# FFN block pairs of a two-block transformer kernel: seven half-width products in place of eight for the last eight pairs of eleven

## Chip, cores and metric

One core of one Trainium2 chip. The metric is the device time of one launch in microseconds, the median over runs. A TensorE clock has two levels here, 1.2 and 2.4 GHz; the profile gives the granted share of the upper.

## What is computed

The reference runs 512 tokens of width 1024 in float32 through two transformer blocks: a hybrid mixer, cross attention and an FFN, then an FFN, a recurrent mixer, cross attention and an FFN again. Three stages have the form that the change touches:

```python
def rms_norm(x, g):
    y = x * lax.rsqrt(jnp.mean(x * x, axis=-1, keepdims=True) + EPS)
    return y * g
def swiglu(h, w_gate, w_up, w_down):        # w_gate, w_up: 1024 x 2816, w_down: 2816 x 1024
    return (silu(h @ w_gate) * (h @ w_up)) @ w_down
# fa: x = x + swiglu(rms_norm(x)); fb, fc: x = x + 0.5 * swiglu(rms_norm(x))
```

## The kernel before

Everything is kept transposed: a tile has 128 features on the partitions and the 512 tokens along the row. Float32 accuracy comes from splitting each operand into a high part in a rounded format (`whi`, `xh`, `hh`) and the rest (`wlo`, `xl`, `hl`); each product is three matmuls, high x high, high x low and low x high, all issued at line 1170 and summed in one PSUM bank.

The weights pass in slots of 256 rows by 512 columns through four buffers each of `raw`, `whi` and `wlo`. `load` (line 2917) fetches a slot on SP's queue, `w_hi` on ScalarE rounds it (line 1541 is the helper that records it), `w_lo` on VectorE subtracts (helper line 2030). Python code writes one order list, `ORDER`, from which each engine's program is made; `gemm` (line 405) runs over the slots of one weight group and its four output tiles, `point` and `soon` (lines 367 and 363) place the work of the other engines between the matmul groups, and `Counts` turns each event into a semaphore value. PSUM has eight banks: `main` (0 to 3) for the large products and `side` (4 to 7) for the rest.

An FFN stage (`ffn`, line 935) has eleven block pairs. Pair i takes 256 gate and 256 up columns: four slots, four output tiles, 2 x 3 matmuls of 512 columns in each. `ffn_gate` on VectorE (line 2500) multiplies the gate sum by `R`, the norm factor of each token; ScalarE (line 1884) takes the Silu; GpSimd (line 2842, helper 2764) multiplies by `R` once more for the up half; `ffn_up` on VectorE (line 2508) multiplies by the up sum; ScalarE (line 1889) and `h_lo` (line 2515) split the hidden tile. Two products of 22 deep tiles, `d0` and `d1`, bring it back to width 1024; `residual` adds them to `xT`. The gain is folded into `xh` and `xl`, and `R` of a stage comes from squares, a sum on GpSimd and two small TensorE products (line 1265) in its first pair. In fb the residual stream itself is normalised as well, by `x_scaled` (line 2521).

The printed code below also shows the memory projections' weight groups (`mkv1`, `mkv2`), whose tokens are 256 and whose matmuls therefore have 256 columns.

## Time and profile before

| what | us |
|---|---|
| timed runs | 2422.54, 2423.30, 2423.92 (median 2423.3) |
| profiled execution, span from first to last instruction | 2420.5 |
| mean granted TensorE clock | 0.998 |
| busy: TensorE, VectorE, ScalarE, GpSimd | 2397.5, 1263.9, 1002.5, 331.9 |
| the three FFN stages in the chain | 362.3, 353.2, 347.1 |
| DMA traffic | 251.65 MB, mean 104 GB/s |

The profiled execution is a fourth one; of it the profile gives the span, and no time around the span is listed. In the views, PE is TensorE's matmuls and PEld its weight loads (they overlap matmuls), DVE is VectorE, ACT ScalarE, POOL GpSimd, SPq SyncE's DMA queue. A matmul's printed duration reaches into the next one; its cost is the distance between starts. "idle before" is the engine's idle time ahead of a group and what ended it.

### The profile page before, as it was taken

How to read it: one execution, taken by the hardware profiler on the slowest of the kernel's cores; microseconds unless marked ns; L12 is line 12 of the kernel's file. 1: busy time of each engine (PE TensorE's matmuls, PEld its weight loads, DVE VectorE, ACT ScalarE, POOL GpSimd, SP SyncE). 2: the span in 40 equal slices, each digit the busy share in tenths (PEclk: the TensorE clock that was granted, in tenths of full speed). 3: DMA queues.
4: the chain of work that ended last, by engine and by line, in shares of the span. 5: the costliest groups of instructions: out<-in, count | busy, mean ns of one | idle time of the engine just before them, and what ended most of it. 6: DMA issues, size and time to landing. Idle time of an engine off the chain costs nothing.

```text
span 2420.5 us, 30412 instructions
## 1 busy us (share of the span) xinstructions
PE 2397.5 (99%) x12064; PEld 1956.4 (81%) x12064; DVE 1263.9 (52%) x1907; ACT 1002.5 (41%) x1634; POOL 331.9 (14%) x258
## 2 busy tenths in 40 slices
PE   8999999999999999999999999999999999999998
PEld 7777778777898888888888888888887888888887
DVE  5688746468765455443333544333678555333422
ACT  7766654234563344333223433222644454323321
POOL 0000000555100100111102111101032201101100
PEclk9999999999999999999999999999999999999999
DMA  6221235323665232332323332332322232333231
GB/s 203 71 70 51 86 99 183 113 68 108 200 210 209 96 105 70 105 95 88 96 97 101 99 97 90 96 100 88 111 63 63 87 113 74 101 96 105 97 100 56
DMA packets 172638, 251.65 MB, mean 104 GB/s; under 512 B 11472, under 2 KB 90576, under 8 KB 172496
## 3 DMA queue, kind: packets, MB, share of 16 engines
q1 hardware_dynamic: 171344, 248.13, 32.5%
q8 instruction: 95, 1.56, 0.3%
q10 hardware_dynamic: 1152, 1.57, 0.2%
q14 instruction: 47, 0.39, 0.1%
HBM read 231.83 MB, written 16.78 MB: 103 GB/s over the span
## 4 chain that ended last, share of the span: by engine, by line
PE 96%; DVE 2%; ACT 1%; issue 0%; POOL 0%; DMA 0%; DVEq 0%; SPq 0%; POOLq 0%
PE bank L1170 94%; PE bank L1299 1%; DVE wlo L2030 0%; PE bank L1322 0%; DVE T L2038 0%; PE bank L1447 0%; PE bank L1423 0%; DVE macc L2030 0%; PE bank L1265 0%; DMA raw<-in_w_in 0%; DVE xg L2034 0%; ACT whi L1541 0%; DVE ml L2038 0%; DVE bank L2336 0%; DVE W L2030 0%
## 5 line engine op out<-in xcount | busy, mean ns | idle before, releaser
L1170 PE MATMUL bank<-xh,whi 128*128 128x512 f32 x1784 | 710.1, 398 | 8.0 <-DVE wlo L2030 8.0
L1170 PE MATMUL bank<-xh,wlo 128*128 128x512 f32 x1784 | 696.6, 390 | 0.0
L1170 PE MATMUL bank<-xl,whi 128*128 128x512 f32 x1784 | 695.9, 390 | 0.0
L2030 DVE TENSOR_TENSOR wlo<-raw,whi 128x1024 fp32r<-128x1024 f32 (+2 forms) x406 | 500.2, 1234 | 337.2 <-ACT whi L1541 337.0
L1541 ACT ACTIVATE whi<-raw 128x1024 fp32r<-128x1024 f32 (+2 forms) x406 | 419.2, 1038 | 513.7 <-PE bank L1170 507.2
L1170 PEld LDWEIGHTS bank<-xh,whi 128*128 128x128 f32 x1784 | 335.7, 188 | 94.7 <-issue 20.2
L1170 PEld LDWEIGHTS bank<-xh,wlo 128*128 128x128 f32 x1784 | 335.4, 188 | 71.1
L1170 PEld LDWEIGHTS bank<-xl,whi 128*128 128x128 f32 x1784 | 336.0, 188 | 65.4
L2030 DVE TENSOR_TENSOR T<-bank,R 128x512 f32<-128x512 f32 x86 | 59.0, 687 | 344.3 <-PE bank L1170 344.3
L1170 PE MATMUL bank<-hh,whi 128*128 128x512 f32 (+1 forms) x536 | 206.9, 386 | 0.0
L1170 PE MATMUL bank<-hl,whi 128*128 128x512 f32 (+1 forms) x536 | 206.8, 386 | 0.0
L1170 PE MATMUL bank<-hh,wlo 128*128 128x512 f32 (+1 forms) x536 | 206.8, 386 | 0.0
L2764 POOL TENSOR_TENSOR T<-T,R 128x512 f32<-128x512 f32 x66 | 94.0, 1424 | 618.6 <-ACT T L1887 618.6
L1887 ACT ACTIVATE T<-T 128x512 f32<-128x512 f32 x66 | 41.7, 632 | 235.0 <-DVE T L2030 235.0
L1170 PEld LDWEIGHTS bank<-hh,whi 128*128 128x128 f32 x536 | 100.7, 188 | 20.5
L1170 PEld LDWEIGHTS bank<-hh,wlo 128*128 128x128 f32 x536 | 100.7, 188 | 20.4
L1170 PEld LDWEIGHTS bank<-hl,whi 128*128 128x128 f32 x536 | 100.7, 188 | 20.0
L2764 POOL TENSOR_TENSOR acc<-acc,T 128x512 f32<-128x512 f32 (+1 forms) x43 | 62.9, 1462 | 227.0 <-ACT T L1595 170.9
L1170 PE MATMUL bank<-whi,xh 128*128 128x512 f32 (+1 forms) x192 | 90.2, 470 | 0.0
L2764 POOL TENSOR_TENSOR xw<-xg,sm 128x512 f32<-128x512 f32 x24 | 28.6, 1201 | 446.1 <-DVE T L2030 421.0
L2785 POOL COPY acc<-T 128x512 f32<-128x512 f32 x8 | 5.5, 692 | 553.1 <-ACT T L1595 553.1
L1784 ACT ACTIVATE E<-bank,sm 128x128 f32<-128x128 f32 x128 | 40.0, 365 | 95.0 <-DVE bank L2336 72.4
(356 smaller groups left out, 3494.9 us busy)
## 6 DMA issues: line engine op xcount, KB each, us to landing
raw<-in_w_in SPq DMA_DIRECT2D x92, 512.0 KB, 3.6
raw<-in_w_ffn_in SPq DMA_DIRECT2D x88, 256.0 KB, 3.2
raw<-in_ffn_gate SPq DMA_DIRECT2D x88, 256.0 KB, 2.8
raw<-in_ffn_up SPq DMA_DIRECT2D x88, 256.0 KB, 3.1
raw<-in_ffn_down SPq DMA_DIRECT2D x44, 512.0 KB, 3.6
raw<-in_w_ffn_out SPq DMA_DIRECT2D x22, 512.0 KB, 3.6
raw<-in_w_xattn_kv SPq DMA_DIRECT2D x16, 512.0 KB, 4.4
raw<-in_w_kv_mem SPq DMA_DIRECT2D x16, 512.0 KB, 4.9
```

What stands on the lines that cost most here:

```text
L1170: return e.matmul(out, l, r, start=start, stop=stop, skip_group_check=skip)
L1299: ins = e.transpose(b[:, chunk(r)], p[:, r, chunk(j)], ident)
L1541: return e.activation(out, in_, ACT.Copy)
L1784: ins = e.activation(E[n % 3][:, c, :], b[:, chunk(j)], ACT.Exp, bias=nac[:, c, 32 + n:33 + n])
L1887: e.activation(t[:], t[:], ACT.Silu).then_inc(*up("ffn_silu", ("ffn silu", tag, j)))
L2030: return e.tensor_tensor(out, a, b, op)
L2764: return e.tensor_tensor(out, a, b, op)
L2785: e.tensor_copy(sums[:, 0:width], t[:, 0:width]).then_inc(*up("sum_pool", ("sum", tag, k), ("tmp", "free", n)))
```

## The change

The first three pairs of each stage (`PLAIN`) stay as they are. For the other eight, weights (1024 x 512 for gate and up together) are cut in two by output columns (128 and 128 of each tile pair) and in two by depth (even and odd tiles of 128), tokens in two halves of 256. The eight quarter products are then had from seven, with sums of weight quarters and of token quarters as operands and the products summed in PSUM in a shared order.

- Weights: a quarter (`quarter`, 1 MB, gate and up, one depth parity) is loaded by two DMAs (`load_quarter`). VectorE forms four combinations a pair (`w_sum`), ScalarE and VectorE split seven operands of 1024 elements a partition (`s_hi`, `s_lo`).
- Tokens: `operands` builds, during the three plain pairs, seven token operands of 256 columns in high and low form for each of four depth pairs (`x_gain`, `x_norm`, `x_sum`, `op_hi`, `op_lo`). They hold gain and `R`, so nothing is multiplied by `R` afterwards, and GpSimd has no part in these pairs.
- Products: `product` runs 2 x 4 x 3 matmuls of 256 columns. The order (`product_order`) weaves a pair's last three among the next pair's first four. Product 1 is copied from bank a to bank b (`seed_b`), so that two sums go on from it; a second copy (`seed_f`) follows product 7; products 5 and 6 are kept in SBUF (`keep`) and added later (`c22`, `c12`). Pairs alternate between the `main` and `side` banks and between two rings of four temporary tiles.
- Silu and multiplication go by quarters of 256 tokens (`s_silu`, `s_mul`) into `hid`. The split of all 22 hidden tiles (`split_h`) moves from the pairs to the end of the products and into `d0`; `x_scaled` moves into `d0`.
- The GpSimd DMA scratch is 1 KB, so all tiles start lower in SBUF. `hh`, `hl`, `quarter`, `shi`, `slo` and `xop` share space with `xh`, `xl`, `raw`, `whi` and `wlo`, which adds waits at the start and end of the products.

```diff
-        hh = [at_kb(118 + 2 * j, [P, S], F32R, name="hh") for j in range(22)]
-        hl = [at_kb(162 + 2 * j, [P, S], F32R, name="hl") for j in range(22)]
+        HH = [218, 96, 98, 100, 102] + [162 + 2 * j for j in range(17)]
+        hid = [at_kb(118 + 2 * j, [P, S], name="hid") for j in range(22)]
+        hl = [at_kb(118 + 2 * j, [P, S], F32R, name="hl") for j in range(22)]
+        hh = [at_kb(kb, [P, S], F32R, name="hh") for kb in HH]
+        quarter = [at_kb(kb, [P, 2, 4, 256], name="quarter") for kb in (0, 8, 72, 80)]
+        wsum = [at_kb(kb, [P, 2, 4, P], name="wsum") for kb in (88, 92)]
+        shi = [at_kb(16 + 4 * i, [P, 2, 4, P], F32R, name="shi") for i in range(NH)]
+        slo = [at_kb(32 + 4 * i, [P, 2, 4, P], F32R, name="slo") for i in range(NH)]
+        xop = [at_kb(162 + 14 * i, [P, 14, 256], name="xop") for i in range(4)]
+        xopr = [at_kb(162 + 14 * i, [P, 14, 256], F32R, name="xopr") for i in range(4)]
 
...
+        def product_order():
+            order = [(PLAIN, p) for p in (1, 5, 6, 2)]
+            for i in range(PLAIN + 1, 11):
+                order += [(i - 1, 7), (i, 1), (i - 1, 4), (i, 5)]
+                order += [(i - 1, 3), (i, 6), (i, 2)]
+            return order + [(10, 7), (10, 3), (10, 4)]
+        PRODUCTS = product_order()
+        PLACE = {x: n for n, x in enumerate(PRODUCTS)}
+        COMBINED = {5: 0, 6: 1}
...
+        def seven_finished(tag, i, p):
+            if p == 1:
+                step("seed_b", tag, i)
+            elif p in (5, 6):
+                step("keep", tag, i, p)
+            elif p == 2:
+                step("s_silu", tag, i, 11)
+                soon(0, "s_mul", tag, i, 11)
+            elif p == 7:
+                step("seed_f", tag, i)
+                step("c22", tag, i)
+                soon(0, "s_silu", tag, i, 22)
+                soon(1, "s_mul", tag, i, 22)
+            elif p == 4:
+                step("s_silu", tag, i, 21)
+                soon(0, "s_mul", tag, i, 21)
+            elif p == 3:
+                step("c12", tag, i)
+                soon(0, "s_silu", tag, i, 12)
+                soon(1, "s_mul", tag, i, 12)
+        def prepare_sum(tag, n):
+            if n < len(PRODUCTS) and PRODUCTS[n][1] in (5, 6, 7):
+                step("w_sum", tag, *PRODUCTS[n])
+        def prepare_last(tag, n):
+            if n < len(PRODUCTS) and PRODUCTS[n][1] == 3:
+                step("w_sum", tag, *PRODUCTS[n])
+        def prepare_hi(tag, n):
+            if n < len(PRODUCTS):
+                step("s_hi", tag, n)
+                soon(0, "s_lo", tag, n)
...
+        def split_h(tag, j):
+            step("h_hi", tag, j)
+            soon(0, "h_lo", tag, j)
+        def begin_seven(tag):
+            def hook(n):
+                if n == 4:
+                    for i in range(PLAIN, 11):
+                        for e in range(2):
+                            step("quarter", tag, i, e)
+                if n in (11, 13, 15):
+                    prepare_hi(tag, (n - 11) // 2)
+                if n in (12, 14):
+                    prepare_sum(tag, n // 2 - 5)
+            return hook
+        def seven(tag):
+            first = SEVEN[tag] + len(PRODUCTS)
+            ready[0] = loaded[0] = first
+            upto[0] = min([x for x in SEVEN.values() if x > first] + [NS])
+            for n, (i, p) in enumerate(PRODUCTS):
+                ring = seven_ring(i)[0]
+                if p == 1:
+                    for b, letter in enumerate("aebf"):
+                        ring.new(letter, tag, i, among=(b,))
+                    for b, what in enumerate(("even", "odd", "c22", "u2")):
+                        (tmp2 if i % 2 else tmp).new(what, tag, i, among=(b,))
+                step("product", tag, n)
+                pay()
+                owed.append(lambda i=i, p=p: seven_finished(tag, i, p))
+                point()
+                prepare_sum(tag, n + 4)
+                prepare_last(tag, n + 6)
+                prepare_hi(tag, n + 3)
+                if (i, p) == (8, 5):
+                    split_h(tag, 0)
+                if n >= PLACE[9, 3] + 3:
+                    split_h(tag, n - PLACE[9, 3] - 2)
+                if n + 3 >= len(PRODUCTS):
+                    split_to(first + n + 4 - len(PRODUCTS))
+            step("mark", f"{tag}d")
...
+            drain(built[0])
+            seven(tag)
+            for x, j in enumerate(range(4, 22)):
+                soon(max(0, 2 * x - 2), split_h, tag, j)
+            if tag == "fb":
+                for k in range(8):
+                    soon(4 + 4 * k, "x_scaled", k)
...
+            def product(tag, n):
+                i, p = PRODUCTS[n]
+                c = SEVEN[tag] + n
+                h, l = shi[c % NH], slo[c % NH]
+                letter = {1: "a", 2: "a", 5: "e", 3: "e", 6: "b", 7: "b", 4: "f"}[p]
+                hi, lo = {1: (11, 4), 2: (12, 5), 3: (13, 6), 4: (10, 3), 5: (7, 0), 6: (9, 2), 7: (8, 1)}[p]
+                u, b = seven_bank(letter, tag, i)
+                w.wait_ge(*at("w lo", c))
+                if p in (1, 5):
+                    ring, name = seven_ring(i)
+                    w.wait_ge(*free(ring, name, u))
+                elif p in (2, 6):
+                    w.wait_ge(*at("seed b", tag, i))
+                elif p == 7:
+                    w.wait_ge(*at("kept", tag, i, 6))
+                elif p == 4:
+                    w.wait_ge(*at("seed f", tag, i))
+                else:
+                    w.wait_ge(*at("kept", tag, i, 5))
+                for gu in range(2):
+                    out = b[:, 256 * gu:256 * gu + 256]
+                    for k in range(4):
+                        w.wait_ge(*at("op lo", tag, k, 0 if hi > 10 else 1))
+                        a, d = h[:, gu, k, :], l[:, gu, k, :]
+                        t, tl = xopr[k][:, hi, :], xopr[k][:, lo, :]
+                        mm(out, a, t, p in (1, 5) and gu == 0 and k == 0, False, skip=True)
+                        mm(out, a, tl, False, False, skip=True)
+                        ins = mm(out, d, t, False, k == 3, skip=True)
+                ins.then_inc(*up("gemm", ("product", tag, i, p), ("w used", c)))
...
+            def op_hi(tag, kp, part):
+                t, tr = xop[kp], xopr[kp]
+                if part == 0:
+                    w.wait_ge(*at("x norm", tag, kp))
+                    ins = copy(tr[:, 11:14, :], t[:, 8:11, :])
+                else:
+                    w.wait_ge(*at("x sum", tag, kp))
+                    w.wait_ge(*at("op lo", tag, kp, 0))
+                    ins = copy(tr[:, 7:11, :], t[:, 0:4, :])
+                ins.then_inc(*up("x_hi", ("op hi", tag, kp, part)))
+            def s_hi(tag, n):
+                i, p = PRODUCTS[n]
+                c = SEVEN[tag] + n
+                if p in (1, 2, 4):
+                    w.wait_ge(*at("quarter", tag, i, 0 if p == 1 else 1))
+                else:
+                    w.wait_ge(*at("w sum", tag, i, p))
+                w.wait_ge(*at("w used", c - NH))
+                copy(eight(shi[c % NH][:]), part_of(tag, i, p)).then_inc(*up("w_hi", ("w hi", c)))
+            def seed_b(tag, i):
+                ring, name = seven_ring(i)
+                u, b = seven_bank("b", tag, i)
+                w.wait_ge(*free(ring, name, u))
+                w.wait_ge(*at("product", tag, i, 1))
+                copy(b[:], seven_bank("a", tag, i)[1][:]).then_inc(*up("x_exp", ("seed b", tag, i)))
+            def keep(tag, i, p):
+                name, n, t = seven_tile("c22" if p == 5 else "u2", tag, i)
+                w.wait_ge(*free(tmp2 if i % 2 else tmp, name, n))
+                w.wait_ge(*at("product", tag, i, p))
+                copy(t[:], seven_bank("e" if p == 5 else "b", tag, i)[1][:]).then_inc(*up("x_exp", ("kept", tag, i, p)))
+            def seed_f(tag, i):
+                ring, name = seven_ring(i)
+                u, f = seven_bank("f", tag, i)
+                w.wait_ge(*free(ring, name, u))
+                w.wait_ge(*at("product", tag, i, 7))
+                copy(f[:], seven_bank("b", tag, i)[1][:]).then_inc(*up("x_exp", ("seed f", tag, i)))
...
+            def x_norm(tag, kp):
+                t = xop[kp]
+                w.wait_ge(*at("R", "fb2" if tag == "fb" else tag))
+                w.wait_ge(*at("x gain", tag, kp))
+                r0, r1 = (R[:, o:o + 256].unsqueeze(1).to_broadcast([P, 2, 256]) for o in (0, 256))
+                tt(t[:, 8:10, :], t[:, 8:10, :], r0, ALU.mult)
+                tt(t[:, 7:11:3, :], t[:, 7:11:3, :], r1, ALU.mult).then_inc(*up("x_lo", ("x norm", tag, kp)))
+            def x_sum(tag, kp):
+                t = xop[kp]
+                w.wait_ge(*at("x norm", tag, kp))
+                tt(t[:, 0:2, :], t[:, 7:8, :].to_broadcast([P, 2, 256]), t[:, 8:11:2, :], ALU.subtract).then_inc(
+                    *up("x_lo", ("x first", tag, kp)))
+                w.wait_ge(*at("x first", tag, kp))
+                tt(t[:, 2, :], t[:, 10, :], t[:, 0, :], ALU.subtract).then_inc(*up("x_lo", ("x second", tag, kp)))
+                w.wait_ge(*at("x second", tag, kp))
+                tt(t[:, 3, :], t[:, 9, :], t[:, 2, :], ALU.subtract).then_inc(*up("x_lo", ("x sum", tag, kp)))
...
+            def w_sum(tag, i, p):
+                out = part_of(tag, i, p)
+                w.wait_ge(*at("quarter", tag, i, 0))
+                w.wait_ge(*at("quarter", tag, i, 1))
+                if p in COMBINED:
+                    if i == PLAIN:
+                        w.wait_ge(*at("w used", G[f"{tag}{PLAIN - 1}"]["ids"][1]))
+                    else:
+                        w.wait_ge(*at("w hi", slot_of(tag, i - 1, p)))
+                        w.wait_ge(*at("w lo", slot_of(tag, i - 1, p)))
+                        w.wait_ge(*at("w sum", tag, i - 1, 6 if p == 5 else 3))
+                if p == 5:
+                    ins = tt(out, part_of(tag, i, 7), part_of(tag, i, 4), ALU.add)
+                elif p == 6:
+                    w.wait_ge(*at("w sum", tag, i, 5))
+                    ins = tt(out, part_of(tag, i, 5), part_of(tag, i, 1), ALU.subtract)
+                elif p == 7:
+                    w.wait_ge(*at("w sum", tag, i, 5))
+                    ins = tt(out, out, part_of(tag, i, 1), ALU.subtract)
+                else:
+                    there = slot_of(tag, i, 5 if i == 10 else 2)
+                    w.wait_ge(*at("w hi", there))
+                    w.wait_ge(*at("w lo", there))
+                    w.wait_ge(*at("w sum", tag, i, 6))
+                    ins = tt(out, part_of(tag, i, 2), part_of(tag, i, 6), ALU.subtract)
+                ins.then_inc(*up("w_lo", ("w sum", tag, i, p)))
+            def s_lo(tag, n):
+                i, p = PRODUCTS[n]
+                c = SEVEN[tag] + n
+                w.wait_ge(*at("w hi", c))
+                tt(eight(slo[c % NH][:]), part_of(tag, i, p), eight(shi[c % NH][:]).bitcast(F32), ALU.subtract).then_inc(
+                    *up("w_lo", ("w lo", c)))
+            def c22(tag, i):
+                t = seven_tile("c22", tag, i)[2]
+                u, b = seven_bank("b", tag, i)
+                w.wait_ge(*at("kept", tag, i, 5))
+                w.wait_ge(*at("seed f", tag, i))
+                tt(t[:], b[:], t[:], ALU.add).then_inc(*up("ffn_in", ("c22", tag, i), (seven_ring(i)[1], "free", u)))
+            def c12(tag, i):
+                t = seven_tile("u2", tag, i)[2]
+                u, x = seven_bank("e", tag, i)
+                w.wait_ge(*at("kept", tag, i, 6))
+                w.wait_ge(*at("product", tag, i, 3))
+                tt(t[:], x[:], t[:], ALU.add).then_inc(*up("ffn_in", ("c12", tag, i), (seven_ring(i)[1], "free", u)))
...
+            def load_quarter(tag, i, e_):
+                r = quarter_of(i, e_)
+                ids = G[f"{tag}{PLAIN - 1}"]["ids"]
+                before = [(j, x) for j in range(PLAIN, 11) for x in range(2) if (j, x) < (i, e_) and quarter_of(j, x) == r]
+                if before:
+                    for event in quarter_done(tag, *before[-1]):
+                        w.wait_ge(*event)
+                elif r > 1:
+                    w.wait_ge(*at("w used", ids[2 * r - 3]))
+                else:
+                    for c in ids:
+                        if c % NR // 2 == r:
+                            w.wait_ge(*at("w hi", c))
+                            w.wait_ge(*at("w lo", c))
+                for gu, (src, c0) in enumerate(SOURCE[tag]):
+                    e.dma_start(quarter[r][:, gu, :, :], src[:, c0 + 256 * i:c0 + 256 * i + 256].rearrange(
+                        "(k e p) n -> p k e n", e=2, p=P)[:, :, e_, :]).then_inc(
+                        *up(f"mx{r}", *([("quarter", tag, i, e_)] if gu else [])))
 
...
```

## Rows read from the trace of the kernel before

**Rows 1.** The page: span, busy time of each engine, granted clock by slice, chain

```profile
span 2420.5 us, 30412 instructions
PE 2397.5 (99%) x12064; PEld 1956.4 (81%) x12064; DVE 1263.9 (52%) x1907; ACT 1002.5 (41%) x1634; POOL 331.9 (14%) x258
...
PEclk9999999999999999999999999999999999999999
...
PE 96%; DVE 2%; ACT 1%; issue 0%; POOL 0%; DMA 0%; DVEq 0%; SPq 0%; POOLq 0%
```

**Rows 2.** The chain in order of time (start us, us, what), the FFN stages

```profile
985.50 362.28 PE bank L1170 x1606
...
1354.13 353.23 PE bank L1170 x1562
...
2064.01 347.12 PE bank L1170 x1560
```

**Rows 3.** Timeline of TensorE in an FFN block (start us, us, engine, line, operation)

```profile
1000.11 0.39 PE L1170 MATMUL bank<-xh,wlo 128*128 128x512 f32 x1
...
1002.83 0.39 PE L1170 MATMUL bank<-xh,wlo 128*128 128x512 f32 x1
```

**Rows 4.** Timeline of TensorE in the memory projections, 256 columns

```profile
625.33 0.28 PE L1170 MATMUL bank<-ml,whi 128*128 128x256 f32 x1
...
627.97 0.28 PE L1170 MATMUL bank<-mh,wlo 128*128 128x256 f32 x1
```

**Rows 5.** Timeline of TensorE's weight loads beside rows 4

```profile
625.33 0.19 PEld L1170 LDWEIGHTS bank<-mh,wlo 128*128 128x128 f32 x1
625.45 0.19 PEld L1170 LDWEIGHTS bank<-mh,whi 128*128 128x128 f32 x1
```

**Rows 6.** Timeline of VectorE at the end of an FFN block

```profile
1017.12 1.22 DVE L2030 TENSOR_TENSOR wlo<-raw,whi 128x1024 fp32r<-128x1024 f32 x1
1018.25 0.68 DVE L2030 TENSOR_TENSOR hl<-T,hh 128x512 fp32r<-128x512 f32 x1
1018.86 1.22 DVE L2030 TENSOR_TENSOR wlo<-raw,whi 128x1024 fp32r<-128x1024 f32 x1
```

**Rows 7.** Groups of VectorE by form (busy us, mean ns, idle before)

```profile
L2030 DVE TENSOR_TENSOR wlo<-raw,whi 128x1024 fp32r<-128x1024 f32 x394 | 493.2, 1254 | 331.2 <-ACT whi L1541 331.0
L2030 DVE TENSOR_TENSOR T<-bank,R 128x512 f32<-128x512 f32 x86 | 59.0, 687 | 344.3 <-PE bank L1170 344.3
L2038 DVE SCALAR_TENSOR_TENSOR xl<-xT,vec,xh 128x512 fp32r<-128x512 f32 x48 | 52.7, 1106 | 4.9 <-ACT xh L1542 4.9
L2336 DVE COPY_PREDICATED bank<-cst,bank 128x256 f32<-128x256 int32 x64 | 26.8, 420 | 1.7 <-PE bank L1170 1.6
```

**Rows 8.** Groups of ScalarE by form

```profile
L1541 ACT ACTIVATE whi<-raw 128x1024 fp32r<-128x1024 f32 x394 | 412.7, 1053 | 510.4 <-PE bank L1170 505.3 <-DMA raw<-in_w_branch_ssd 4.7
L1541 ACT ACTIVATE hh<-T 128x512 fp32r<-128x512 f32 x66 | 41.6, 630 | 24.5 <-DVE T L2030 24.5
L1541 ACT ACTIVATE pt<-bank 128x512 f32<-128x512 f32 x40 | 23.3, 585 | 17.2 <-PE bank L1299 17.1
L1541 ACT ACTIVATE q<-bank 128x256 f32<-128x256 f32 x16 | 6.0, 378 | 19.8 <-PE bank L1170 19.8
```

**Rows 9.** Groups of GpSimd by form

```profile
L2764 POOL TENSOR_TENSOR T<-T,R 128x512 f32<-128x512 f32 x66 | 94.0, 1424 | 618.6 <-ACT T L1887 618.6
```

**Rows 10.** Busy time by stretch: us, PE, PEld, DVE, ACT, POOL, clock, DMA share, GB/s

```profile
979.30:1348.20 368.90, 368.90 (x1641) 305.83 (x1641) 140.41 (x160) 112.79 (x141) 53.26 (x36) 1.00 0.31 97
640.00:660.00 20.00, 20.00 (x128) 16.77 (x128) 15.74 (x29) 15.15 (x34) 0.40 (x1) 1.00 0.83 265
```

**Rows 11.** DMA issues of the page (count, KB each, us to landing)

```profile
raw<-in_w_ffn_in SPq DMA_DIRECT2D x88, 256.0 KB, 3.2
...
raw<-in_ffn_down SPq DMA_DIRECT2D x44, 512.0 KB, 3.6
```

**Rows 12.** The chain in order of time, memory projections beside the scan

```profile
618.50 60.38 PE bank L1170 x498
```

More of the change, by code:

```diff
@@ L13 @@
 S = 512
-BASE = 17408
+SCRATCH = 1024
+BASE = SCRATCH + 1024
 EPS = 1e-6
@@ L213, in build @@
         tmp = Ring([at_kb(104 + i * 2, [P, S], name="T") for i in range(4)])
+        tmp2 = Ring([at_kb(96 + i * 2, [P, S], name="T2") for i in range(4)])
         zb = Ring([at_kb(kb, [P, S], name="zb") for kb in (154, 156)])
@@ L369, in point @@
             delayed[:] = [[d[0] - 1, d[1]] for d in delayed if d[0]]
-            for d in sorted(due, key=lambda d: d[1][0] != "w_lo"):
+            for d in sorted(due, key=lambda d: d[1][0] not in ("w_lo", "s_lo")):
                 if callable(d[1][0]):
@@ L935, in ffn, with build @@
         def ffn(tag, out):
+            built = []
+            def build():
+                built.append(start(operands(tag), 3))
             if tag == "fb":
@@ L950, in scale @@
                             step("spread", "fb")
-                            for k in range(8):
-                                soon(1 + 2 * k, "x_scaled", k)
                         soon(3, scale)
@@ L956, in ffn, with ahead @@
             else:
-                later(1, norm(tag))
+                def ahead():
+                    norm(tag)()
+                    soon(5, build)
+                later(1, ahead)
             step("mark", f"{tag}")
-            for i in range(11):
+            for i in range(PLAIN):
                 def evict(m, i=i):
@@ L1887, in ffn_gate, with h_hi @@
                 e.activation(t[:], t[:], ACT.Silu).then_inc(*up("ffn_silu", ("ffn silu", tag, j)))
-            def ffn_up(tag, j):
-                n, t = tmp("gate", tag, j)
+            def h_hi(tag, j):
+                w.wait_ge(*at("h done", tag, j))
+                if 0 < j < 5:
+                    for q in (11, 22, 21, 12):
+                        w.wait_ge(*at("s mul", tag, 9, q))
+                elif j > 4:
+                    w.wait_ge(*at("product", tag, 10, 3))
+                copy(hh[j][:], hid[j][:]).then_inc(*up("h_hi", ("h hi", tag, j)))
@@ L2013, in scalar @@
                     "mv_out": mv_out, "kv_split": kv_split, "xq_out": xq_out, "x_scores": x_scores, "x_turn": x_turn, "x_pv": x_pv, "ffn_gate": ffn_gate,
-                    "ffn_up": ffn_up, "bounds": bounds, "f_sig": f_sig, "f_log": f_log, "h_silu": h_silu,
+                    "h_hi": h_hi, "x_gain": x_gain, "op_hi": op_hi, "s_hi": s_hi, "seed_b": seed_b, "keep": keep, "seed_f": seed_f,
+                    "s_silu": s_silu, "bounds": bounds, "f_sig": f_sig, "f_log": f_log, "h_silu": h_silu,
                     "i_out": i_out, "u_first": u_first, "b_split": b_split, "level": level, "ends": ends, "ke_turn": ke_turn,
@@ L2747, in vector @@
                     "ffn_gate": ffn_gate, "ffn_up": ffn_up, "h_lo": h_lo, "x_scaled": x_scaled, "residual": residual,
+                    "x_norm": x_norm, "x_sum": x_sum, "op_lo": op_lo, "w_sum": w_sum, "s_lo": s_lo, "c22": c22, "c12": c12, "s_mul": s_mul,
                     "bounds": bounds, "f_out": f_out, "f_gate": f_gate, "f_log": f_log, "h_out": h_out,
```

169 lines of the change are left out of this document (141 added, 28 removed).

## The prediction

> **What bounds the kernel now.** I read the page first. TensorE is busy for 99% of a span of 2420.5 us, its granted clock stands in the top tenth in all forty slices, and 96% of the chain that ended last is TensorE's own [rows 1]. The chain in order of time then shows the three feed-forward (FFN) stages, fa, fb and fc, as unbroken runs of TensorE work: 362.3, 353.2 and 347.1 us, with nothing but norm matmuls between them [rows 2]. So in these stages only TensorE's own work counts, and whatever takes from it is gained one for one until another engine makes it wait.
>
> What one matmul costs must be read from starts, since the page's means (some 390 ns) overlap. In an FFN block a matmul of 512 columns starts every 2.72/12 = 0.2267 us [rows 3]. Where the moving operand has 256 columns, in the memory projections, one starts every 2.64/22 = 0.120 us [rows 4], and each has its own weight load, started at the same distance [rows 5]. A half-width matmul thus costs 53% of a full one, not 50%: 106.7 ns for 256 columns at the granted full level of 2.4 GHz and 13.3 ns beside it; 213.3 and 13.3 for 512.
>
> **TensorE's part.** A block pair (256 gate and 256 up columns, 1024 deep, 512 tokens) is now 4 weight slots x 4 output tiles x 2 x 3 = 96 matmuls of 512 columns, 96 x 0.2267 = 21.76 us. In the new form it is 7 products x 2 (gate, up) x 4 deep tiles x 3 = 168 matmuls of 256 columns, 168 x 0.120 = 20.16 us. That is 7/8 of the columns (6144 fewer, 2.56 us) with 72 more of the fixed 13.3 ns (0.96 us): 1.60 us less. Eight pairs in each of three stages: 24 x 1.60 = 38.4 us.
>
> The Trainium skill's page "TensorE: Matmul & The Clock Gate", section "Back-to-back issue gap", gives N/2.4 + 2.5 ns a matmul, so 215.8 and 109.2 ns; by it, as an estimate, a pair would gain 2.37 us and all of them 57 us. The rows have 226.7 and 120.0, and the measurement decides.
>
> **What must keep pace.** Each product waits for a high and low half of its own weight combination (`s_hi` on ScalarE, `s_lo` on VectorE), and four of seven for a combination that VectorE first adds up (`w_sum`).
> - VectorE, per pair: four `w_lo` of 1024 elements, two `ffn_gate` and two `ffn_up` go, two `h_lo` move to the down product; seven `s_lo`, four `w_sum` (all 1024 elements), `c22` and `c12` (512) and four `s_mul` (256) come. From start to start a 1024-element operation takes 1.13 us and a 512-element one 0.61 [rows 6]; 256 elements I put at 0.34 (0.61 less the 0.27 us between the 687 and 420 ns forms [rows 7]). 11 x 1.13 + 2 x 0.61 + 4 x 0.34 = 15.0 us of 20.16, 74%. Taken with the full mean durations, 11 x 1.254 + 2 x 0.69 + 4 x 0.42 = 16.9 us, 84%. The sums read 128-column pieces, which no row shows; I take the plain price.
> - ScalarE, per pair: seven `s_hi`, four copies of 512 (`seed_b` and `seed_f` from bank to bank, `keep` twice out of PSUM) and four Silu of 256 come, four `w_hi`, two Silu of 512 and two `h_hi` go or move. 7 x 1.053 + 4 x 0.585 + 4 x 0.378 = 11.2 us, 56% [rows 8]. No row has ScalarE writing PSUM. Bounds: the 585 ns of reading PSUM, and twice it; I take 0.6 us, as writing PSUM costs VectorE nothing unusual, 420 ns for 256 elements [rows 7].
> - GpSimd loses two multiplications by R a pair (1424 ns each), and with them the hop VectorE, ScalarE, GpSimd, VectorE at each eviction. It is off TensorE's path, so it gives nothing [rows 9].
> - Loads: the bytes are the same, 2 MB a pair, in 1 KB pieces as before; the FFN stage draws 97 GB/s with the DMA engines 31% busy, while another stretch of this kernel draws 265 [rows 10].
>
> **Do the waits bite?** I followed the order list by products of 2.88 us. `s_lo` of product n+2 stands in VectorE's queue behind only what product n-1's end releases, so it has nearly two products to run; the dearest such turn holds `c22` (0.6 us, and up to 0.9 us until `seed_f` has landed), one `s_lo` and one `w_sum`, 3.8 us, and the next two are short (1.5 and 2.6). A seed or a kept copy always has one whole product between what it reads and who needs it (6, then 2, then 7; 7, then 1, then 4): 2.88 us against about 1 us, even 1.5 with the dear copy. A quarter of weights (1 MB, two DMAs on SP's queue) comes free about 8.5 products into a pair's life and the sum that reads its successor comes at 12: 3.5 products or 10 us. SP's sixteen quarters a stage stand in one queue, each waiting in turn. A 256 KB piece lands in 3.2 us and one of 512 KB in 3.6 [rows 11]; two of these, even one after the other, are 7.2 us. If the quarter were late, `w_sum` would block VectorE and the `s_lo` behind it, with two more products before TensorE feels it. Steady state: no stall, 0 us.
>
> **Edges, three times each.** Token operands: four groups of scaling, sums and splits, 3840 elements on VectorE and 2816 on ScalarE each, so about 4 x 4.3 = 17 and 4 x 2.9 = 12 us, spread over the three plain blocks (65 us), where VectorE is busy 38% and ScalarE 31% of the time [rows 10]: hidden. At their price uncovered this would be 17 us a stage. Entry: the second pair's last quarter can only load once the last plain block has left `xl` and `xh`, and its first sum comes 3 products (8.6 us) on against at most 7.2: hidden by 1.4 us. Exit: the first down slot's `w_lo` runs in the last product behind `c12`: 0.2 + 0.6 + 1.13 us against 2.88, thin. The 18 remaining splits of hidden tiles (0.63 us on ScalarE, 0.61 on VectorE [rows 6, 8]) come about ten matmul groups ahead of use within 60 us of the first down product; the move of `x_scaled` there adds 8 x 0.8 us to VectorE and is hidden the same way. I take 0.6 us an edge pair, about 2 us in all; bounds 0 and 10.
>
> Sum against the profiled span: 2420.5 - 38.4 + 2 = 2384.1 us. The median of the runs, 2423.3, lies 2.8 us above that span, so 2386.9; I say 2387. Less than 0.2%, about 5 us, can't be told from no change here.
>
> **Rivals.**
> 1. The hand-overs bite. What would do it is a copy into PSUM while TensorE writes a neighbouring bank, or a VectorE queue that runs behind. The trace of before has no such copy and no such chain. At 0.2 to 1.3 us a pair the gain shrinks by 5 to 31 us: 2392 to 2418, middle 2400. A 0.1 us hole a product would already be 17 us. Chance 0.17.
> 2. VectorE becomes the bound and the kernel is slower. The place is the eleven 1024-element operations a pair. With the waits in the queue (about 2 us of `seed_f` and Silu landings) and 2.6 us of short ones, a pair exceeds the old 21.76 us when each costs over (21.76 - 4.6)/11 = 1.56 us. The mean today is 1.254 at longest [rows 7] and only `xl`'s operations of 512 elements show such slowness beside GpSimd work (1106 ns mean where 512 elements usually take 690). At 1.8 us a pair takes 24.4 us: + 2.6 x 24 = 63, so 2486. For it speaks the unseen strided read; against it that GpSimd falls silent in just these blocks. Chance 0.06.
> 3. Weight loads show. The load counts 188 to 192 ns in the trace [rows 5] and there are 168 where 96 were; if they ran one behind another a pair would take 31.6 us and the kernel 2423.3 + 24 x 9.8 = 2659 us. Against it: rows 5 have loads starting each 0.12 us, and 498 matmuls in 60.4 us (0.121 each) ran unbroken in the chain [rows 12], so neither loads nor instruction supply fail at that rate. Chance 0.02. The Trainium skill's page "TensorE: Matmul & The Clock Gate", section "Measured speedup vs the span model", says a load overlaps a matmul in flight only where the row group differs; by it this rival would hold. The trace disagrees: in rows 4 and 5 loads on all 128 rows start together with matmuls.
> 4. The change doesn't do what it says in time: the half-width gain is eaten to within 5 us of nothing (1.4 to 1.8 us of stall a pair, or an entry and exit stall of 10 to 13 us a stage). Chance 0.04.
>
> The forecast itself, 2383 to 2391, has 0.71.
>
> **Numbers.** Faster: forecast and rival 1, 0.88. Same 0.04, slower 0.08 (rivals 2, 3). The range runs from 2382 (edges free, pitch 0.1195 as the shortest 256-column stretches allow, 2 us) to 2402, which takes in the forecast and the better half of rival 1, and leaves out some 0.18.
>
> **What would show it.** Right: 4032 matmuls of 256 columns with `xop` as moving operand, 0.120 us apart; VectorE 70 to 85% busy in those stretches, ScalarE 50 to 60%; the chain still one run of TensorE per stage, some 12.8 us shorter each; pair to pair 20.2 us. Rival 1: idle of TensorE before `xop` matmuls released by ScalarE's `bank<-bank` copies. Rival 2: the same released by `slo`, with VectorE above 95%. Wrong altogether: a matmul pitch off 0.120, a granted clock below full, or `quarter` loads at the head of the waits.

## The result and the profile after

The changed kernel takes 2385.36 us (median, 2385.11 to 2385.97), the kernel before 2422.92 in the same comparison: ratio 0.9846, 95% interval 0.9832 to 0.9860. The forecast was 2387 in a range of 2382 to 2402. The profiled execution took 2385.45 us in all, 1.85 us more than its span.

The page after, for [rows 1]:

```profile
span 2383.6 us, 34351 instructions
PE 2359.7 (99%) x13792; PEld 2007.5 (84%) x13792; DVE 1525.4 (64%) x2207; ACT 1167.8 (49%) x1910; POOL 266.8 (11%) x210
...
PEclk9999999999999999999999999999999999999999
...
PE 95%; DVE 3%; ACT 1%; issue 1%; DMA 0%; POOL 0%; SPq 0%; DVEq 0%; POOLq 0%; ACTq 0%
```

TensorE is as full as before, with 1728 more matmuls and less time; VectorE rises from 52 to 64%, ScalarE from 41 to 49%. The chain in order of time, for [rows 2] (start us, us, what):

```profile
986.72 349.50 PE bank L1349 x2182
...
1342.57 44.93 PE bank L1349 x198
...
1388.38 2.32 DVE wsum L2314
...
1392.74 0.49 ACT bank L1751
1393.23 0.14 issue
1393.37 290.01 PE bank L1349 x1892
```

```profile
2039.88 334.35 PE bank L1349 x2136
```

Stage fa went from 362.28 to 349.50 us and fc from 347.12 to 334.35: 12.78 and 12.77 less, where eight pairs at 1.60 us are 12.8. Stage fb, from norm to norm, went from 353.67 to 341.25, 12.42 less: its chain leaves TensorE once, at 1387.5 us, for a sum on VectorE and what follows it on ScalarE. The three make 38.0 us. The span fell by 36.9; the other 1.1 us were lost ahead of fa, which the last experiment looks into.

The new matmuls (groups of the page, busy us and mean ns, and TensorE's timeline in a product, for [rows 4]):

```profile
L1349 PE MATMUL bank<-xopr,shi 128*128 128x256 f32 x2688 | 484.1, 283 | 0.1
...
L1349 PE MATMUL bank<-xopr,slo 128*128 128x256 f32 x1344 | 380.3, 283 | 0.0
```

```profile
1100.07 0.28 PE L1349 MATMUL bank<-xopr,slo 128*128 128x256 f32 x1
1100.18 0.40 PE L1349 MATMUL bank<-xopr,shi 128*128 128x256 f32 x2
1100.42 0.28 PE L1349 MATMUL bank<-xopr,slo 128*128 128x256 f32 x1
...
1101.51 0.28 PE L1349 MATMUL bank<-xopr,slo 128*128 128x256 f32 x1
```

Between the first and the last line lie twelve matmuls in 1.44 us: 0.120 each. Of the 4029 distances inside the three runs of products, 4019 are 120 ns; only one hole is over 0.1 us, 0.30 us at 1393 us. One pair by the stretches (us, then busy PE, PEld, DVE, ACT, POOL; clock, DMA share, GB/s), and the entry of fa:

```profile
1063.00:1083.16 20.16, 20.16 (x171) 20.16 (x170) 15.22 (x17) 10.67 (x16) 0.00 (x0) 1.00 0.34 105
986.70:1037.80 51.10, 51.10 (x227) 42.29 (x226) 41.09 (x48) 27.22 (x37) 7.75 (x6) 1.00 0.29 93
```

A pair has VectorE busy for 15.22 us of 20.16 (forecast 15.0) and ScalarE for 10.67 (forecast 11.2). The entry of a stage is fuller: 41.1 of 51.1 us on VectorE. A 512 KB piece of a quarter takes 4.6 us in the middle to land, and 3.6 to 7.8 over all 96 of them (forecast 3.6). The groups that answer to [rows 7, 8]:

```profile
L2314 DVE TENSOR_TENSOR slo<-quarter,shi 128x1024 fp32r<-128x1024 f32 x117 | 142.6, 1219 | 2.5 <-ACT shi L1751 2.5
L2314 DVE TENSOR_TENSOR T<-bank,T 128x512 f32<-128x512 f32 x48 | 33.2, 692 | 108.8 <-ACT bank L1751 56.2 <-PE bank L1349 52.7
L2314 DVE TENSOR_TENSOR wsum<-wsum,quarter 128x1024 f32<-128x1024 f32 x24 | 32.5, 1356 | 0.0
L2314 DVE TENSOR_TENSOR wsum<-quarter,quarter 128x1024 f32<-128x1024 f32 x24 | 29.3, 1219 | 0.8 <-PE bank L1349 0.8
```

```profile
L1751 ACT ACTIVATE T<-bank 128x512 f32<-128x512 f32 x48 | 28.7, 598 | 50.6 <-PE bank L1349 50.6
L1751 ACT ACTIVATE bank<-bank 128x512 f32<-128x512 f32 x48 | 28.0, 582 | 37.4 <-PE bank L1349 35.6
```

Reading weight quarters in 128-column pieces costs VectorE nothing (1219 ns), and copying from bank to bank costs ScalarE no more than reading a bank (582 and 598 ns). `T<-bank,T` is `c22` and `c12`: before it VectorE idles 56.2 us in all, 2.3 us a pair, until `seed_f` has landed. That idling costs nothing, as the fourth experiment shows.

### The profile page after: what moved, and what is told of

It reads as the page before. It is cut to its first block, busy times and chain, and to the rows that moved or that the text cites. A ratio compares the mean times of both kernels' runs of the same rounds, so it can differ in the third digit from the quotient of the medians.

```text
span 2383.6 us, 34351 instructions
## 1 busy us (share of the span) xinstructions
PE 2359.7 (99%) x13792; PEld 2007.5 (84%) x13792; DVE 1525.4 (64%) x2207; ACT 1167.8 (49%) x1910; POOL 266.8 (11%) x210
## 4 chain that ended last, share of the span: by engine, by line
PE 95%; DVE 3%; ACT 1%; issue 1%; DMA 0%; POOL 0%; SPq 0%; DVEq 0%; POOLq 0%; ACTq 0%
PE bank L1349 93%; PE bank L1509 1%; DVE wlo L2314 1%; PE bank L1532 0%; DVE T L2322 0%; PE bank L1633 0%; PE bank L1657 0%; DMA zb<-scr_z 0%; DVE macc L2314 0%; PE bank L1475 0%; ACT whi L1751 0%; DMA raw<-in_w_in 0%; DVE ml L2322 0%; DVE xg L2318 0%; DVE bank L2620 0%
## 5 line engine op out<-in xcount | busy, mean ns | idle before, releaser
L1349 PE MATMUL bank<-xopr,shi 128*128 128x256 f32 x2688 | 484.1, 283 | 0.1
L1349 PEld LDWEIGHTS bank<-xopr,shi 128*128 128x128 f32 x2688 | 419.5, 192 | 0.5 <-DVE slo L2314 0.3
L1349 PE MATMUL bank<-xh,whi 128*128 128x512 f32 x1016 | 411.5, 405 | 8.2 <-DVE wlo L2314 8.2
L1349 PE MATMUL bank<-xh,wlo 128*128 128x512 f32 x1016 | 397.9, 392 | 0.0
L1349 PE MATMUL bank<-xl,whi 128*128 128x512 f32 x1016 | 397.2, 391 | 0.0
L1349 PE MATMUL bank<-xopr,slo 128*128 128x256 f32 x1344 | 380.3, 283 | 0.0
L1349 PEld LDWEIGHTS bank<-xopr,slo 128*128 128x128 f32 x1344 | 258.0, 192 | 0.0
L1349 PEld LDWEIGHTS bank<-xh,whi 128*128 128x128 f32 x1016 | 191.5, 188 | 64.7 <-issue 20.2
L1349 PEld LDWEIGHTS bank<-xh,wlo 128*128 128x128 f32 x1016 | 191.3, 188 | 41.7
L1349 PEld LDWEIGHTS bank<-xl,whi 128*128 128x128 f32 x1016 | 191.9, 189 | 35.5
L2314 DVE TENSOR_TENSOR slo<-quarter,shi 128x1024 fp32r<-128x1024 f32 x117 | 142.6, 1219 | 2.5 <-ACT shi L1751 2.5
L2314 DVE TENSOR_TENSOR T<-bank,T 128x512 f32<-128x512 f32 x48 | 33.2, 692 | 108.8 <-ACT bank L1751 56.2
```

The source lines that it names most:

```text
L1349: return e.matmul(out, l, r, start=start, stop=stop, skip_group_check=skip)
L2314: return e.tensor_tensor(out, a, b, op)
```

## The experiments

Each is told by its difference from the changed kernel or the kernel before; the kernel before took 2423.1 to 2423.5 us in each comparison.

**1. What the fixed part of a matmul costs.** The kernel before; in pairs 3 to 10 (a branch of their own in the code) the lines marked + stand in place of those marked -:

```diff
-                        mm(out, a, xh_[k], first, False)
-                        mm(out, a, xl_[k], False, False)
-                        ins = mm(out, c, xh_[k], False, last and kk == 1)
+                        for o in (0, 256):
+                            half = out[:, o:o + 256]
+                            mm(half, a, xh_[k][:, o:o + 256], first and o == 0, False, skip=True)
+                            mm(half, a, xl_[k][:, o:o + 256], False, False, skip=True)
+                            ins = mm(half, c, xh_[k][:, o:o + 256], False, last and kk == 1, skip=True)
```

> The kernel before with each 512-column matmul of pairs 3 to 10 of fa, fb and fc issued as two of 256 columns (same sums, same everything else). It prices the fixed part of a matmul by itself. Theory (a 256-column matmul costs 0.120 us, a 512-column one 0.2267): a pair is 192 x 0.120 = 23.04 us in place of 21.76, so 24 x 1.28 = 31 us more than before, about 2454. Rival, the fixed part is 2.5 ns as the Trainium skill has it: 96 x 24 x 2.5 ns = 6 us more, about 2429. Rival, weight loads of 188 ns show: 192 x 0.188 = 36.1 us a pair, 344 us more.

Measured 2453.18 us, ratio to the kernel before 1.0123 (1.0107 to 1.0138). The stages in its chain:

```profile
984.71 372.54 PE bank L1170 x2374
...
1363.59 363.49 PE bank L1170 x2330
...
2083.80 357.38 PE bank L1170 x2328
```

Each is 10.26 us longer than in [rows 2], together 30.8 where 24 x 1.28 = 30.7 were due. So 2304 more matmuls cost 13.4 ns each over their columns, where the forecast had 13.3. The figure of 2.5 ns is excluded for this kernel, and so are weight loads that show.

**2. Gain per pair or cost per stage.** `PLAIN = 3` becomes `PLAIN = 7`.

> The changed kernel with seven plain pairs and four in seven products (half as many). It tells gain per pair from cost per stage. Theory (1.60 us a pair, edges near nothing): 12 x 1.60 = 19.2 us less than before, about 2404; that is 19 us slower than the changed kernel. Rival, a cost of each stage's entry and exit that is paid back by a larger gain a pair: the time lies above the middle of the two kernels, at 2407 or more. Nothing below 2402.

Measured 2404.96 us, ratio to before 0.9922 (0.9906 to 0.9939). The stages are 355.90, 346.85 and 340.75 us, 6.38, 6.38 and 6.37 less than before: 1.60 a pair again, and nothing left for a cost of entry and exit. The rival falls.

**3, 4. How much room VectorE has.** Some `s_lo` are done twice, with a wait between:

```diff
+                for r_ in range(1 if True else 0):        # fourth experiment: if p in (2, 4, 5, 6)
+                    tt(eight(slo[c % NH][:]), part_of(tag, i, p), eight(shi[c % NH][:]).bitcast(F32), ALU.subtract).then_inc(
+                        *up("again_lo", ("again lo", c, r_)))
+                    w.wait_ge(*at("again lo", c, r_))
                 tt(eight(slo[c % NH][:]), part_of(tag, i, p), eight(shi[c % NH][:]).bitcast(F32), ALU.subtract).then_inc(
```

> The changed kernel with each of the seven s_lo of a pair done twice (same result). VectorE's work a pair goes from 15.2 us (its busy time in 20.16 us of the profile) to 15.2 + 7 x 1.25 = 24 us, above TensorE's 20.16. Theory (VectorE is hidden with room of about 5 us a pair, less what it idles waiting in its queue): a pair now takes 24 to 26 us, so 24 x (3.8 to 5.8) = 91 to 140 us more, 2476 to 2525, and VectorE is over 92% busy in these stretches. If VectorE mattered not at all: no change.

Measured 2474.81 us, 89.5 more than the changed kernel, ratio to before 1.0211 (1.0196 to 1.0227): just under the expected 2476. The three runs of products take 190.5, 191.4 and 190.5 us in place of 161.2 to 161.5, 23.8 a pair. In the steady part (stretch, columns as above):

```profile
1080.00:1160.00 80.00, 72.19 (x563) 68.34 (x562) 79.18 (x81) 35.93 (x53) 0.00 (x0) 1.00 0.26 80
```

VectorE is busy 99% of the time, and the holes between TensorE's product matmuls (what each start comes later than 120 ns after the one before) add up to 90.3 us, which covers the 89.5 lost. The pair time is VectorE's sum from start to start: fourteen `s_lo` at 1.20 us (2.40 for two in the timeline below), four sums at 1.13, 2 x 0.61 and 4 x 0.34 make 23.9.

```profile
1103.32 2.48 DVE L2314 TENSOR_TENSOR slo<-quarter,shi 128x1024 fp32r<-128x1024 f32 x2
1105.72 0.42 DVE L2314 TENSOR_TENSOR hid<-bank,T 128x256 f32<-128x256 f32 x1
```

So an engine that has become the bound no longer idles for others: the 2 us of queue waits that I had added are not there.

> The changed kernel with four of the seven s_lo of a pair done twice (products 2, 4, 5, 6). VectorE's work is 15.2 + 4 x 1.25 = 20.2 us a pair, just TensorE's 20.16. It measures how much of VectorE's idle time can really be used. Theory: with up to 2 us a pair lost in its queue waiting for seed_f and Silu results, a pair takes 20.2 to 22.2 us, so 0 to 48 us more than the changed kernel, 2385 to 2433; I take 2405. No change at all would mean that the waits cost VectorE nothing once it runs late.

Measured 2393.67 us, 8.3 more than the changed kernel and far below the 2405 that I took. The steady part takes it without a hole:

```profile
1063.00:1083.16 20.16, 20.16 (x170) 20.16 (x170) 20.02 (x22) 10.69 (x16) 0.00 (x0) 1.00 0.34 106
```

VectorE is busy for 20.02 of 20.16 us and TensorE loses nothing. The holes of over 0.2 us lie in the first 14 us of products of each stage (in fa 1.3 us at 1044.5 and 0.6 at 1048.8, in fb 2.0, 1.8 and 0.6). The room in a steady pair is the whole difference of 4.9 us; the entry has less. In fb the chain to the first of these holes passes through a load of weights, for which the first sum stands idle 2.14 us:

```profile
1379.56 8.02 DMA quarter<-in_ffn_up
...
1387.66 0.06 DVE wsum L2314
```

**5, 6. How much room the hand-overs have.** The copies of `seed_b`, `seed_f` and `keep` are done twice, then four times, as in:

```diff
+                for r_ in range(1):        # sixth experiment: range(3)
+                    copy(b[:], seven_bank("a", tag, i)[1][:]).then_inc(*up("again_act", ("again b", tag, i, r_)))
+                    w.wait_ge(*at("again b", tag, i, r_))
                 copy(b[:], seven_bank("a", tag, i)[1][:]).then_inc(*up("x_exp", ("seed b", tag, i)))
```

> The changed kernel with each copy of seed_b, seed_f and keep done twice before it is signalled (same result), so each hand-over takes about 0.7 us longer: 1.2 to 1.3 us after the product. Theory (each hand-over has a whole product of 2.88 us): no change, 2385 within 1. Rival, hand-overs are on the edge: 24 x 2 x up to 0.7 us = up to 34 us more.

Measured 2387.05 us (2386.82 to 2388.08), 1.7 more, so just outside the "within 1". The one hole over 0.1 us in its products is again in fb's entry, 1.08 us where the changed kernel has 0.30; where the rest of the 1.7 lies was not followed. fa and fc take 349.50 and 334.35 us, to the digit those of the changed kernel.

> The changed kernel with each of these copies done four times. A hand-over takes 4 x 0.6 and some 0.2 us for waits between, 2.6 to 2.9 us after the product, the limit of 2.88; ScalarE's work goes from 10.7 to about 18.5 us a pair. Theory: this is where the hand-over begins to bite at products 7 and 4, 0 to 1 us a pair, 0 to 24 us more, 2385 to 2409; idle of TensorE, if any, stands before xopr matmuls and is ended by ScalarE's copies.

Measured 2394.04 us, 8.7 more. In the steady part:

```profile
1080.00:1160.64 80.64, 80.64 (x672) 80.54 (x671) 61.82 (x70) 69.13 (x109) 0.00 (x0) 1.00 0.33 105
```

ScalarE works 86% of the time and TensorE is still full. The large holes stand again in the entries only (1.0 and 0.8 us in fa and fc, 2.5 and 0.8 in fb); smaller ones add up to about 2 us over all. The place that I had expected, products 7 and 4 in every pair, was wrong: four copies in a row take 2.42 us there and end 0.26 us before the product that needs them starts (1177.25 and 1177.51 us, for instance), so even they do not bite.

**7. Sums on GpSimd.** `w_sum` moves, unchanged, from VectorE's functions to GpSimd's and signals a semaphore of its own:

```diff
-                ins.then_inc(*up("w_lo", ("w sum", tag, i, p)))        # in the VectorE functions
+                ins.then_inc(*up("w_sum", ("w sum", tag, i, p)))       # in the GpSimd functions
```

> The changed kernel with the four w_sum of a pair on GpSimd. GpSimd takes about 2 x 1.3 us for 1024 elements, 10.4 us a pair, and VectorE falls to 10.7 us. Theory A, the engines work beside each other: each sum has four products to be ready in, so no change, 2385 within 2. Theory B, they hold each other up (in fb's entry a sum took 2.31 us in place of 1.22 while GpSimd multiplied in 2.06 in place of 1.30): GpSimd's and VectorE's times add to 21 us and more for 20.16, so 1 to 3 us a pair, 24 to 72 us more, 2410 to 2457, and the slo operations show well over 1.22 us.

Measured 2392.50 us, 7.1 more than the changed kernel, ratio to before 0.9872 (0.9857 to 0.9887): between the two theories. Groups, timelines of both engines, and the steady pair:

```profile
L2314 DVE TENSOR_TENSOR slo<-quarter,shi 128x1024 fp32r<-128x1024 f32 x117 | 230.8, 1988 | 13.9 <-ACT shi L1751 13.8
...
L2314 DVE TENSOR_TENSOR T<-bank,T 128x512 f32<-128x512 f32 x48 | 33.0, 687 | 69.5 <-PE bank L1349 54.9 <-ACT bank L1751 14.6
```

```profile
1067.19 3.20 POOL L3123 TENSOR_TENSOR wsum<-quarter,quarter 128x1024 f32<-128x1024 f32 x1 [0.25 <-DMA quarter<-in_w_ffn_in]
...
1073.70 2.59 POOL L3123 TENSOR_TENSOR quarter<-quarter 128x1024 f32<-128x1024 f32 x1
```

```profile
1066.92 1.22 DVE L2314 TENSOR_TENSOR slo<-quarter,shi 128x1024 fp32r<-128x1024 f32 x1
...
1073.95 3.42 DVE L2314 TENSOR_TENSOR slo<-quarter,shi 128x1024 fp32r<-128x1024 f32 x1
1077.30 0.41 DVE L2314 TENSOR_TENSOR hid<-bank,T 128x256 f32<-128x256 f32 x1
```

```profile
1063.00:1083.16 20.16, 20.16 (x171) 20.16 (x170) 17.64 (x15) 10.42 (x15) 11.36 (x4) 1.00 0.36 112
```

The mechanism of theory B is there: the `slo` that starts at 1073.95 beside a GpSimd sum takes 3.42 us in place of 1.22, and ends about one `slo` after the sum does (1076.3). It matters who starts first. Of the 117 `slo<-quarter` operations, the 49 that begin inside a GpSimd operation take 3.42 us in the middle, while the 5 that are under way when one begins (1066.92) keep 1.21; there the GpSimd sum is the longer one, 3.20 us where those that meet no such operation take 2.41. What reads one operand from PSUM keeps its time: 21 of the 48 `T<-bank,T` begin inside a GpSimd operation and take 692 ns. The Trainium skill's "GPSIMD Engine Reference", section "1. Specifications", says that GpSimd shares its SBUF interfaces with VectorE and contends with VectorE instructions that have two SBUF inputs. The trace agrees. What theory B had wrong is the sum: it still fits. VectorE's own 10.3 us (15.22 less four sums) and GpSimd's 11.4 overlap enough for a pair of 20.16 us without a hole. The 7 us are again in the entries, 1.7 us in fa and fc and 2.4 in fb, where the pause is followed by a stretch at a granted clock of 0.79 (1395 to 1403 us).

**8. The cover of the token operands.** The build's rate of 3 becomes 0.01, so that it runs after the plain pairs.

> The changed kernel with the token operands built only after the third plain pair's matmuls, none beside them. It prices the cover that the plain pairs give. Theory: four groups of 4.3 us on VectorE and 2.8 us on ScalarE, partly waiting for each other, so 17 to 25 us in which TensorE stands still in each stage, of which perhaps 5 us more are lost to a lower granted clock: 50 to 85 us more, 2435 to 2470. If the products could start on the first group and go on as the others come, it would be less, 20 us a stage or under.

Measured 2471.24 us, 85.9 more, ratio to before 1.0199 (1.0182 to 1.0216), at the upper end. fa's chain at one of the groups, and the stretch:

```profile
1059.57 1.42 ACT xop L1752 x3
1060.99 0.02 issue
1061.01 1.31 DVE xop L2314 x2
...
1063.95 0.88 DVE xopr L2314
1064.83 0.04 issue
1064.87 1.22 PE bank L1349 x4
```

```profile
1036.00:1070.00 34.00, 9.36 (x46) 7.97 (x45) 27.61 (x35) 16.87 (x25) 2.03 (x1) 0.60 0.10 31
```

TensorE stands 8.8, 5.6, 5.7 and 5.7 us for the four groups, 25.8 a stage, and 77 in all. It runs for the first products between them at the lower level: 62 of its 256-column matmuls start 213 or 214 ns apart in place of 120, 5.8 us more. My price of the uncovered build, 17 us a stage, counted VectorE alone; a group goes back and forth between ScalarE and VectorE and costs its latency.

**9. One more pair.** Two plain pairs:

```diff
-        PLAIN = 3
+        PLAIN = 2
-            return e if i % 2 else 2 + e
+            return 2 + e if i % 2 else 1 - e
-                built.append(start(operands(tag), 3))
+                built.append(start(operands(tag), 5))
```

> The changed kernel with two plain pairs and nine in seven products; the token operands are spread over two plain pairs at rate 5 in place of 3, and even pairs take the raw area for their quarters, odd ones the xh area. Three more pairs in seven products give 3 x 1.6 = 4.8 us, if the entry stays hidden: 2380.5. Theory: it does not. In the changed kernel VectorE is busy 41.1 of the 51.1 us from fa's norm to the first product; without one plain pair's some 9.5 us of its work 31.6 us are left for 29.3 us, so each stage's entry stands still for 2 to 6 us: 2387 to 2399, slower than the changed kernel though still well under the kernel before.

Measured 2410.11 us (2407.61 to 2411.17), ratio to before 0.9944 (0.9932 to 0.9957). The direction was right and the size was not: 24.8 us more than the changed kernel, so some 30 us of pauses against 4.8 gained, 10 a stage and not 2 to 6. The stretches of fa's entry:

```profile
986.00:1016.00 30.00, 29.36 (x130) 23.97 (x128) 24.21 (x33) 18.16 (x27) 2.84 (x2) 1.00 0.28 91
1016.00:1030.00 14.00, 7.81 (x48) 7.19 (x48) 11.80 (x13) 5.93 (x8) 3.06 (x2) 0.88 0.31 107
```

VectorE is busy for 24.2 of the first 30 us. From its first operation on a token operand (987.63) to the second product (1024.13, due at 1018.1) it works 30.1 of 36.5 us; the rest is mostly waits for ScalarE, 1.18 us twice between two halves of a group and 1.99 us for an `s_hi`. So VectorE's work alone nearly fills the time, as I had counted, and the waits of one group's steps for each other come on top, which I had not. How much of the pauses is due to each is not shown. Pauses of over 0.7 us before products are 7.5, 6.8 and 5.9 us in the three stages; in fb the chain already leaves TensorE in the plain pairs. How the rest divides between that and the lower clock is not itemised.

**10. The layout alone.** The kernel before with `BASE` at 2048 and the GpSimd DMA scratch at 1 KB.

> The kernel before with only the smaller GpSimd DMA scratch, so that all tiles lie 15 KB lower. In the changed kernel's trace the part ahead of fa ends 1.2 us later than before, 1 us of it at a transfer of z from memory. Theory: this is chance of the transfers, not the addresses, so no difference from the kernel before, 2423 within 1.5. Rival: the layout costs it, 2424 to 2425.

Measured 2423.56 us against 2423.12, ratio 1.0000 (0.9991 to 1.0009): the runs show no difference and would not show 1 us. The traces do. In all ten with the low layout the chain passes through one transfer of z:

```profile
648.15 6.88 DMA zb<-scr_z
```

and in neither of the two with the old layout. This profile's span is 2422.2 us, 1.7 above that of before. That says little, since the spans of the kernel before alone reach from 2420.2 to 2423.0 us. The stretch that holds the transfer, from about 618 to 680 us, says more: it takes 60.6 and 60.8 us with the old layout and 61.0 to 62.3 in the ten with the low one. So my "chance of the transfers" is the less likely reading, for 0.8 of the 1.2 us by which fa starts later; the other 0.4 lie ahead of 618 us, where the traces of either layout differ by about 1 us among themselves. Why the layout would delay a transfer stays open.

## Why the prediction was right

- The main term, 24 x 1.60 us, was exact: 12.78 and 12.77 us in the stages without a pause, and 1.60 a pair at four pairs too. It rested on starts and not on durations. Taken by the page's mean durations (283 and 390 ns) the change would have looked like a loss: 168 x 283 against 96 x 390 ns, 47.5 against 37.4 us.
- The formula of the Trainium skill's page "TensorE: Matmul & The Clock Gate", section "Back-to-back issue gap", gave 57 us as an estimate. The rows won, and experiment 1 shows by itself the fixed part, 13.4 ns a matmul where the formula has 2.5.
- VectorE 15.0 and ScalarE 11.2 us a pair became 15.22 and 10.67; the two unseen prices, strided sums and copies into PSUM, came out at the plain ones (1219 and 582 ns).
- "Steady state: no stall" held, with more room than was claimed. Experiments 4 and 6 took VectorE to 99% and ScalarE to 86% of a pair without a hole.
- The term of the edges was mis-sized: 2 us put, 0.4 measured, all of it in fb. It was also misplaced. I called the exit "thin" (`w_lo` behind `c12`); no hole is there in any stage. The thin place is the entry, in VectorE's queue: with the sum of product 6 running beside GpSimd's last multiplication by R,

```profile
1386.99 1.47 DVE L2314 TENSOR_TENSOR slo<-wsum,shi 128x1024 fp32r<-128x1024 f32 x1 [1.06 <-ACT shi L1751]
1388.38 2.31 DVE L2314 TENSOR_TENSOR wsum<-wsum,quarter 128x1024 f32<-128x1024 f32 x1
```

```profile
1387.55 2.06 POOL L3151 TENSOR_TENSOR T<-T,R 128x512 f32<-128x512 f32 x1 [0.17 <-ACT T L2097]
```

  the sum takes 2.31 us in place of 1.22 and the `s_hi` and `s_lo` behind it come late. So does the copy `seed_b`, which stands behind that `s_hi` in ScalarE's queue; it is the last thing that product 6 waits for (1392.74 in the chain above). The sign of rival 1 is there after all, for 0.30 us. Three of 24 such sums are lengthened (their mean is 1356 ns against 1219), one in each stage; in fa it starts at 1038.20 us, with the first product, in fb 1.1 us behind the first product, and only there it reaches TensorE. My step "GpSimd is off TensorE's path, so it gives nothing" holds for the time gained, and missed this cost.
- In fa and fc the lengthened sum makes no pause. What fb has besides is a late load of weights:

```profile
1383.51 1.23 DVE L2314 TENSOR_TENSOR wsum<-quarter,quarter 128x1024 f32<-128x1024 f32 x1 [0.76 <-PE bank L1349]
```

  This first sum of fb starts 3.8 us before the first product, in fa and fc 5.5 us. The view puts its wait down to TensorE, but TensorE had long been done with what this sum needs of it, as fa and fc show. In the traces of the changed kernel and of experiments 5 and 6 it starts 0.43 us after its second quarter has landed (1383.08 here) each time, though that falls at a different point of TensorE's work. The code says why the load is late: slots take the four buffers in turn, fb's begin two further on than fa's and fc's, and so its first quarter has to wait for the last two plain slots. It is issued 12.0 us before the first product, in fa 23.7, and the second quarter stands behind it in the queue. The prediction priced the load of the second pair's last quarter and not this one, and took 3.6 us for a piece where 4.6 is the middle. That the pause is due to the late load and the lengthened sum together is read from the traces; a kernel that moves either alone was not tried.
- The slowness beside GpSimd could have been seen in the trace of before. I read the mean of `wlo`, 1254 ns, and wrote that only `xl`'s operations show it; but `wlo` has 1219 ns in the middle and 2317 at most, and the 25 of 1024 elements that begin inside a GpSimd operation take 1.77 us in the middle.
- Against the profiled span: 2384.1 forecast, 2383.6 measured. The edges came 1.6 us cheaper and the part ahead of fa 1.1 us dearer, which was not foreseen; that the two nearly cancel is luck. In the median the forecast missed by 1.6 us (2387 against 2385.4), and 1.0 of it is the step from span to median: I put 2.8 us, but the time around a span is about 1.8 us in every run of the later comparisons (2422.35 against 2420.6, for instance), and the rest of the 2.8 was that the profiled execution of before was a short one.
- Rival 1 (hand-overs) fell for the steady pairs by experiments 5 and 6, rival 3 (weight loads) by experiment 1, and rival 4 by the measured time. The sentence on loads and row groups that rival 3 cites stands in that page's section "The mechanism", not in "Measured speedup vs the span model". What the range leaves out by these chances is 0.20 and not 0.18. Rival 2 (VectorE) is real, and its point was put about right: VectorE's start-to-start sum over 20.16 us a pair costs one for one, as experiment 3 shows. I had added 2 us of queue waits to it, which an engine that runs late doesn't have.

## What to carry to other kernels

Price a change of matmul width from starts in the trace at the new width, fixed part included: seven products of half width for eight give a saving of 7.4% here, not 12.5%, and all of it arrives as long as each helper engine's start-to-start sum stays below TensorE's for the same stretch. Look for the danger where a pipeline begins: there VectorE has the last plain tiles, the operands and the first weights at once, and the added work of experiments 4 to 7 cost time there and next to none in the steady pairs. Look at each stage's own entry, too: the same code gave fb its first weights 11.7 us later than fa. What has to be built before a stage costs its latency across engines and not its busy time where nothing covers it (25.8 us against 17 in experiment 8), and so needs cover of at least that length.

## What was not expected of the hardware

- A VectorE operation with two SBUF operands that begins inside a GpSimd one ends about 1.1 us after it: 3.42 us in place of 1.22 beside a 2.59 us sum. One that was under way first keeps its 1.2 us, and so do operations with one operand in PSUM their 692 ns (experiment 7).
- A VectorE queue that idled 4.5 us a pair for results of others took 4.8 us of further work a pair without a trace of delay: 20.02 of 20.16 us busy.
- Moving all tiles 15 KB lower went with one transfer of z on the chain in ten traces of ten, and with 0.2 to 1.7 us more for that stretch than in the two traces of the old layout.
